# Rotations behind a projection's last rows, gates between the latent norms' steps, a new first stage, and modulation steps moved

## The reference, cut to what matters

```
def adaln(c, w, b):                      # shift, scale, gate (twice in the second block)
    return split(silu(c) @ w + b)        # w: 1024 x 6144 in the second block, 1024 x 3072 in the first
h = rmsnorm(x) * g * (1 + scale) + shift
q, k = rope(h @ w_q), rope(h @ w_k)      # "even" layer of the first block; rotations of q and k
cq = rmsnorm(h @ w_cq); ckv = rmsnorm(h @ w_ckv)       # "odd" layer: two latent vectors with norms
q = cq @ w_qb;  k, v = ckv @ w_kvb;  gate = silu(h @ w_gm)
x = x + g_m * (gate * attention(q, k, v)) @ w_out
x = x + g_f * (silu(h @ wg) * (h @ wu)) @ wd           # second block only
```

## Time and profile before

| | us |
|---|---|
| median of 3 runs (2638.52 to 2640.34) | 2638.56 |
| profiled execution, device time | 2641.35 |
| its span | 2639.6 |
| PE busy in the span | 2372.5 |
| DVE busy | 1290.1 |
| ACT busy | 780.2 |
| POOL busy | 403.9 |

### The profile page before, as it was taken

How to read it: one execution, slowest core, us unless ns; L and a number is a source line. 1 busy time by engine, 2 the same in 40 slices (tenths; PEclk the granted TensorE clock), 3 DMA queues, 4 the chain that set the end, 5 groups by cost and what they waited for, 6 DMA issues and landing times.

```text
span 2639.6 us, 30486 instructions
## 1 busy us (share of the span) xinstructions
PE 2372.5 (90%) x11834; PEld 1805.6 (68%) x11834; DVE 1290.1 (49%) x2860; ACT 780.2 (30%) x1607; POOL 403.9 (15%) x377
## 2 busy tenths in 40 slices
PE   5789998989899998989998989999969788999996
PEld 5676566558545756777875768887757557788875
DVE  4546564651135445628567356664226962333322
ACT  1235201430111302622237322223323361222332
POOL 1320010002100121031010120003541003000154
PEclk9989999989899998999879999999969899999998
DMA  6110232000124063013410035553213101222221
GB/s 276 48 41 18 88 106 94 17 17 0 68 86 146 24 181 111 9 64 121 143 66 1 1 128 192 186 183 127 86 48 112 48 1 64 80 96 96 96 96 56
DMA packets 58124, 225.89 MB, mean 86 GB/s; under 512 B 20462, under 2 KB 20974, under 8 KB 41468
## 3 DMA queue, kind: packets, MB, share of 16 engines
q1 hardware_dynamic: 57980, 223.94, 25.4%
HBM read 221.83 MB, written 2.10 MB: 85 GB/s over the span
## 4 chain that ended last, share of the span: by engine, by line
PE 77%; DVE 12%; POOL 3%; ACT 3%; issue 2%; DMA 2%; SPq 0%; POOLq 0%; DVEq 0%; ACTq 0%
PE PS L81 72%; PE PS L86 5%; DVE ACC L110 2%; DVE RINGr L98 1%; DVE WK L103 1%; POOL X L98 1%; DVE WK L152 1%; ACT WK L93 1%; ACT WK L91 1%; POOL WKr L98 1%; DVE WK L137 1%; DVE WK L110 1%; DVE SM L147 1%; DVE WK L98 1%; DMA WK<-in_rpb 1%
## 5 line engine op out<-in xcount | busy, mean ns | idle before, releaser
L81 PE MATMUL PS<-Hr,GBr 128*128 128x512 f32 x1280 | 441.0, 398 | 14.5 <-DVE RINGr L98 6.4
L81 PE MATMUL PS<-Hr,RINGr 128*128 128x512 f32 x1040 | 405.9, 390 | 0.0
L91 ACT ACTIVATE WK<-PS 128x512 f32<-128x512 f32 (+3 forms) x390 | 190.1, 518 | 524.4 <-PE PS L81 322.7
L81 PE MATMUL PS<-H,RING 128*128 128x512 f32 (+1 forms) x928 | 340.2, 518 | 0.0
L110 DVE SCALAR_TENSOR_TENSOR ACC<-ADA,SM,ACC 128x256 f32<-128x256 f32 x616 | 292.7, 499 | 74.7 <-DMA ACC<-in_l_mod_b 31.3
L81 PEld LDWEIGHTS PS<-Hr,GBr 128*128 128x128 f32 x1280 | 242.9, 191 | 73.1 <-POOL Xr L98 9.0
L98 DVE TENSOR_TENSOR RINGr<-RING,GBr 128x1024 fp32r<-128x1024 f32 (+1 forms) x155 | 201.2, 1337 | 184.2 <-ACT GBr L91 184.2
L81 PEld LDWEIGHTS PS<-H,RING 128*128 128x128 f32 x928 | 174.0, 192 | 136.8 <-issue 128.8
L81 PE MATMUL PS<-GBr,WKr 128*128 128x512 f32 (+1 forms) x774 | 249.5, 393 | 14.0 <-POOL WKr L98 12.7
L81 PE MATMUL PS<-RING,GB 128*128 128x256 f32 x1156 | 252.3, 381 | 4.8 <-DVE GB L115 2.2
L86 PE MATMUL PS<-CN,WK 128*128 128x128 f32 (+1 forms) x1152 | 185.9, 303 | 67.2 <-DVE WK L103 52.6
(11 more groups left out here) (175 smaller groups left out, 2911.6 us busy)
## 6 DMA issues: line engine op xcount, KB each, us to landing
ADA<-in_l_mod SPq DMA_DIRECT2D x96, 512.0 KB, 3.9
RING<-in_l_gu SPq DMA_DIRECT2D x44, 1024.0 KB, 4.9
RING<-in_l_wd SPq DMA_DIRECT2D x24, 1024.0 KB, 4.9
RING<-in_l_in SPq DMA_DIRECT2D x17, 1024.0 KB, 4.9
RING<-in_ev_in SPq DMA_DIRECT2D x13, 1024.0 KB, 5.8
ADA<-in_od_ada SPq DMA_DIRECT2D x24, 512.0 KB, 3.6
RING<-in_od_in SPq DMA_DIRECT2D x12, 1024.0 KB, 5.5
RING<-in_l_out SPq DMA_DIRECT2D x8, 1024.0 KB, 5.1
```

Source lines behind the costliest of these rows:

```text
L81: self.last = self.eng.matmul(out, lhsT, rhs, start=start, stop=stop, skip_group_check=True)
L91: self.last = self.eng.activation(out, in_, func, bias=bias, scale=scale)
```

## The change

- **First stage.** The two conditions, padded to 64 columns each, are the stationary operand; PE multiplies all 16 early chunks of shift and scale (groups 0 to 3 of four chunks), 16 matmuls of 256 columns a group, whose results go alternately to the lower and upper 64 partitions. ACT copies a group out, four matmuls with `pick` (two columns) turn it, DVE adds bias and norm gain. The diagonal of the norms replaces the scaled rows and the identity: x^T is a matmul of x with it, and `norm_tile` and the transposes of this stage are gone. The lower 4 column blocks are normalized while PE sums groups 1 and 3. DVE makes the 512 rows, ACT the 256. Loads: the small constants, x, groups 0 and 2, weight chunk 0, the lambda inputs, groups 1 and 3, chunk 1, the big tables, chunks 2 and 3.
- **Rotations** are called once behind both groups; the two `qr` behind the ckv spreads.
- **Odd layer.** ckv and kr come before the first sum of squares; the gate tiles 0 to 3 stand between the norms' steps (tiles 0 and 1 before the spread of cq, 2 before the ckv sums, 3 before kn).
- **Modulation steps.** 24 steps for groups 0 to 3 of the first layer are not in the list any more (they are in the new first stage). Calls: none behind the last vb tiles, none behind gm tile 7, `ada(4)` in proj N behind qd and kd and none behind vd. By the cursor, od group 3 is applied just before the odd layer's norm, and the steps of the second block come up to 12 chunks later: proj I does eight chunks instead of six, two of them behind its last tile.
- **FFN.** POOL's four additions stand behind slices 23, 25, 27 and 29.

```diff
 tensor, fm and fm_split:
                     pe.then_inc(pe_product, ("p", tag, t, s0))
-                    if then is not None:
-                        then(tag, t, s0)
+                if then is not None:
+                    then(tag, t)
...
+            def first_sums(grp):
+                b = next_bank(("first sums", grp), [(act_value, ("first sums", grp))])
+                for j in range(2):
+                    for kh in range(2):
+                        i = grp * 4 + j * 2 + kh
...
+                        for k in range(4):
+                            pe.matmul(half(bank(b, j * 256, j * 256 + 256), k % 2),
+                                      cpad[:, (kh * 4 + k) * 64:(kh * 4 + k) * 64 + 64], wv[:, k, :],
+                                      kh == 0 and k < 2, kh == 1 and k > 1)
+            def first_mods(grp):
+                pe.wait_ge(act_value, ("first sums", grp))
...
+                for f in range(4):
+                    pe.matmul(bank(7, ...), a[:, f * 128:(f + 1) * 128], pick, True, True)
+            def first_turned(f):
+                for gi, tl in enumerate((range(4), range(4, 6))):
...
+                        pe.matmul(bank(b, i * 128, (i + 1) * 128), Xt(t, f * 128, f * 128 + 128), length_at(t), True, True)
+            first_sums(0)
+            first_sums(2)
+            first_mods(0)
+            first_mods(2)
+            pe.wait_ge(x_in, "x")
+            for f in range(4):
+                first_turned(f)
+            first_sums(1)
+            first_turned(4)
+            first_turned(5)
+            first_sums(3)
+            pe.wait_ge(dve_value, ("first mods", 2))
+            first_mods(1)
+            first_mods(3)
+            first_turned(6)
+            first_turned(7)
 vector:
+            def norm_half(f0):
+                for f in range(f0, f0 + 4):
+                    first_norm(f)
+                    if f > f0:
+                        first_lower(f - 1)
+                first_lower(f0 + 3)
+            first_mods(0)
+            first_mods(2)
+            norm_half(0)
...
+            rest(0)
...
+            first_mods(1)
+            first_mods(3)
+            norm_half(4)
 tensor, proj B:
-                ada(4)
+                if j == 0:
+                    ada(4)
 tensor, proj M:
+            gates_m(FIRST["od_gm"], 0)
+            spread("cq", sqw(0, 0, 512), 512, [(dve_value, ("cqn", 1))])
+            fm(FIRST["od_in2"], 8, 0, "gm", 2, gated("gm", 2), LOC, Ht, h_od)
+            ada(3)
+            for key, a0, a1 in halves:
+                sum_squares(key, ...)
...
-                fm(i, 2, 4 + m, "qr", m, roped("qr", m), LOC, cq, cq_ready, rotate)
+                fm(i, 2, 4 + m, "qr", m, roped("qr", m), LOC, cq, cq_ready)
+            for key, a0, a1 in halves:
+                spread(key, ...)
+            for m in range(2):
+                rotate("qr", m)
+            fm(FIRST["od_in2"], 8, 1, "gm", 3, gated("gm", 3), LOC, Ht, h_od)
+            ada(3)
 tensor, proj N:
-                        ada(3)
+                        ada(4)
 gpsimd, ffn:
-                    if fz == 22:
-                        for t in range(4):
-                            add(wd, t, 0, t, WK[:, 6144 + t % 3 * 512:6656 + t % 3 * 512])
+                    if fz > 22 and fz % 2 and fz < 31:
+                        t = (fz - 23) // 2
+                        add(wd, t, 0, t, WK[:, 6144 + t % 3 * 512:6656 + t % 3 * 512])
 sync, proj M:
-            for j in range(4):
-                load()
-            for j in range(4):
-                ada(3)
-                ada(3)
-                load()
+            for loads, steps in ((2, 2), (1, 1), (1, 1), (2, 2), (1, 1), (1, 0)):
+                for j in range(loads):
+                    load()
+                for j in range(steps):
+                    ada(3)
```

More of the change, by code:

```diff
@@ L1036, in ffn @@
                         chunk_done(i)
[L1039 to L1048, removed]
-                        pe.wait_ge(ada_landed(2 * c + k // 4), ("ada_in", 2 * c + k // 4))
-                        pe.matmul(at, wv[k // 4][:, k % 4, f * 128:(f + 1) * 128], cpair[:, 2 * k:2 * k + 2], k == 0,
-                                  k == 7)
@@ L1055, in tensor @@
+            first_turned(7)
+            turn["set"] = list(range(8))
             close(of_pe, "norm ev")
@@ L1500, in scalar, with first_sums @@
                 act.activation(cond_th[key], vec(key, 0, 8), ACT.Tanh, scale=0.5).then_inc(act_value, ("cond", key))
+            act.wait_ge(x_in, "x")
+            for t in range(6):
+                act.activation(H[:, t * 1024:(t + 1) * 1024], Xt(t), ACT.Square, accum=ssq[:, t:t + 1])
+                act.then_inc(act_value, ("sq", "ev", t))
+            def first_sums(grp):
+                act.wait_ge(pe_product, ("first sums", grp))
+                a = ACC[:, grp % 2 * 512:grp % 2 * 512 + 512] if grp < 2 else GATE[:, grp % 2 * 512:grp % 2 * 512 + 512]
+                act.activation(a, bank(where["first sums", grp]), ACT.Copy).then_inc(act_value, ("first sums", grp))
@@ L1508, in scalar @@
-            round_h("ev", ((0, 512), (512, 768)))
+            first_sums(1)
+            first_sums(3)
+            for f in range(4, 8):
+                first_norm(f)
             close(of_act, "norm ev")
-            act.wait_ge(pe_turned, ("end", "norm ev"))
+            act.wait_ge(tables_in, "tables")
             for j in range(2):
@@ L2211, in vector, with gate_m @@
                 copy_out("cq", m, 0, 512)
+            def gate_m(t):
+                gate("gm", t, LOC)
+                if t < 7:
+                    ada(3)
+            for s0, n in ALLT:
+                copy_out("ckv", 0, s0, n)
             diagonal("cq", sqw(0, 0, 512), 512, 256)
+            rope("kr", 0, ALLT)
+            for t in range(2):
+                gate_m(t)
             for k in range(2):
@@ L2237, in vector @@
                 copy_out("vm", t, 0, 512)
-            for t in range(8):
-                gate("gm", t, LOC)
-                ada(3)
+            for t in range(4, 8):
+                gate_m(t)
             close(of_dve, "proj M")
@@ L2642, in gpsimd @@
             rope("kr", 0)
+            for t in range(3):
+                ada(3)
             power(("ckv", 0), n + 1, 4)
@@ L2646, in gpsimd @@
                 rope("qr", m)
-            for t in range(8):
+            for t in range(3, 7):
                 ada(3)
```

242 lines of the change are left out of this document (150 added, 92 removed).

## The result

| | before | after |
|---|---|---|
| median, us (4 runs each on one chip) | 2639.45 (2638.52 to 2643.19) | 2561.39 (2557.42 to 2563.05) |
| ratio to before, 95% interval | | 0.9699 [0.9683, 0.9716] |
| profiled execution; its span | 2641.35; 2639.6 | 2563.00; 2561.2 |

The change is faster by 78 us. The forecast was 2534 (105 less), its range ended at 2556: a miss of 27 us, on the slow side.

What follows compares the result with a forecast made beforehand. PE bounds the kernel gap by gap, with half clock after several gaps and DVE limiting in places. Stage gains less proj I's loss sum to 105.7 us, from 2641.35 to 2535.7; median 2532.9, plus 1 for collisions: 2534, range 2517 to 2556.

Steps and rivals of the forecast that it cites:

- First stage: Start of kernel: sums in alternating halves and new load order start the first projection near 48, not 85.64; gain 38 us.
- Rotations: Even layer's projections: 13 waits of PE for ACT's copy go, with half the restarts; gain 10.7 us.
- End of proj B: Apply and 9.37 us of PE idle go, 1.0 stays, 2 for half clock; gain 12.2 us.
- Proj M: Odd layer: norm and rotation waits, half clock and most end idle go, 2 of new waits; gain 22.4 us.
- FFN additions: Both FFNs: spreading POOL's four additions removes PE's 5.40 wait and 3.4 of half clock; gain 15.6 us in all.
- Proj N: 2.9 us of wait inside goes, end wait 4.67 falls to 0.7, some clock returns; gain 8.8 us.
- Proj S: Apply that waited 4.38 finds its sum, half clock goes, one chunk more for DVE; gain 3.5 us (-3 to 8).
- Proj I: Two more chunks and their loads behind the last tile delay the index scores; loss 5.5 us (4 to 8).
- Rival 5: Whole kernel: the change moves waits and PE only waits elsewhere; half the gain, 2587 us; chance 0.03.
- Rival 2: Proj M's waits replaced by DVE's chunks between norms, 10 us more, proj S at -3: 2551 us; chance 0.15.
- rival 3: First stage 10 us worse and Rival 2's losses in proj M and S together: 2561 us; chance 0.05.

Runs made afterwards that it cites:

- e7: Changed kernel with first-stage conditions padded to 128 columns, all sums in one place, no alternating halves: 2572.1 us.
- e4: Changed kernel with rotations called between a tile's two groups again (qr ones stay behind the ckv spreads): 2573.9 us.
- e1: Changed kernel with every call of the modulation steps back where it was before the change: 2565.1 us.
- e8: Changed kernel with proj M's order of before in all engines, modulation calls still behind gate tiles 0 to 6: 2578.5 us.
- e6: Changed kernel with POOL's four additions in a row behind slice 22 again: 2571.0 us.
- e3: Changed kernel with calls of five steps behind every tile of output projections ev, od, l0, and one instead of two behind proj S's first eight tiles: 2559.7 us.
- e5: Changed kernel with five steps behind tiles 0 to 2 of output projections od and l0 only, one instead of two behind proj S's first eight tiles: 2538.8 us.
- e9: Changed kernel with calls of 3, 3, 1, 0 steps behind proj I's four tiles, the rest in FFN 1: 2556.4 us.
- e10: Changed kernel with no call behind slice 0 of either FFN and calls of 3, 3, 3, 1 steps in proj I: 2555.0 us.
- e12: Kernel of e11 with two steps instead of three behind slice 1 of both FFNs: 2533.9 us.
- e11: Changed kernel with three-step calls behind early od and l0 output tiles, fewer steps in proj S, slice 0 of both FFNs and proj I: 2544.6 us.
- e2: Changed kernel with six steps instead of three behind slices 6, 9 and 12 of FFN 0: 2558.8 us.

## Why the prediction was wrong where it was

**First stage: right.** 37.05 against 38. The halves bring a factor 1.77 / 1.08 = 1.64 a chunk (e7; forecast 1 / 0.56 = 1.8), and the first chunk was there at 13.62, so that the rest followed as drawn: the first projection at 48.59, forecast 48. The Trainium skill ("TensorEngine Tiling (Array Packing)", Theoretical Speedup) allows up to 2 for 64 columns; the trace shows less.

**Rotations: right.** 12.25 against 10.7: the restart of 0.25 counts in full, of which I had taken half. A wait of 1.27 at 264.99 that comes with them (e4) had no term.

**End of proj B: right in size,** 11.4 (e1) against 12.2. The idle time and the apply give 10.2 of it (9.24 + 1.84 less the 0.93 that stay), so about 1.3 is left for the clock, where I had 2.

**Proj M: the sum is right, its two parts are not.** 22.0 against 22.4. The new order gives 17.9 (e8), where I had 10.5 + 6.0 - 2 = 14.5: no wait of PE of more than 0.5 us is left between the norm and the end of the stage, so the 2 kept for new ones were not needed. The steps taken from its end give 3.7 (e1), where I had 7.9. Of those, the 3.0 of half clock lie behind the stage's last mark: 830.50 to 837.30 ran at 0.60 of full before and 749.83 to 756.60 at 1.00 after, 2.7 us, and the table has them in the next stage. That the column agrees to 0.4 is partly luck.

**FFN additions: right by the stages,** 7.2 and 7.4 against 7.8 each. The medians of e6 give 9.6 for both where the forecast had 15.6, so the size is less sure than the place.

**Proj N: over-rated.** The 8.8 are 2.9 inside, 4.0 at the end and 1.9 of clock. The end came (4.67 to 0.93). The 2.9 inside did not go, for the forecast had given no reason why it should: it was 3.76 in the profiled execution, with half clock behind it where the kernel before had none. By the table the miss is 3.1, and about 6 if the 2.7 that belong to proj M's term are taken out. In other executions of the same code the wait is 1.30 to 3.35 (last section), so part of this miss is one execution's. The cause of the wait is a gate group that begins with three chunks, and its bias row: POOL clears ACC for it only at 882.77, behind a mask that had waited 13.28 for its rows. With calls of three steps (e1) PE has two waits there, of 1.16 and 1.15, and the clock reads 1.00 behind them. Timeline of POOL, then DVE, after:

```profile
880.50 2.21 POOL L103 TENSOR_TENSOR WK<-WK,CN 128x960 f32<-128x960 f32 x1 [13.28 <-DMA WK<-in_rpb]
882.77 0.53 POOL L125 MEMSET ACC<- 128x512 f32 x1
```
```profile
886.61 6.07 DVE L115 SCALAR_TENSOR_TENSOR ACC<-ADA,SM,ACC 128x256 f32<-128x256 f32 x8 [11.91 <-DMA ACC<-in_l_mod_b]
```

**Proj S: the step that failed first.** I wrote that the apply "now finds its sum", 3.5 to the good. It was 5.4 to the bad (5.6 come back in e1, with the calls as before). The steps came seven chunks later, and other applies now met chunks just issued: 1.70, 0.70 and 4.86 us of waits and a half-clock stretch. I had counted how many chunks the stage gets (one more) and not which call each apply falls behind. At the last of the three, DVE begins its chunk at 1156.39 and ends it at 1158.44, and PE sums at 1158.49. Its bounds were -3 to 8. e3 and e5 confirm the place: with one step a tile the inner part of proj S is 12.4 us shorter than in the changed kernel.

**FFN 0: a loss I had no term for.** 5.9 us (7.2 less 1.26). It now begins with a gate group of three chunks; e9 makes the same loss in FFN 1 (7.4), e10 moves the wait by a slice, and e12 takes it away from e11 with one chunk fewer in the call.

**Proj I: right mechanism, under-rated.** 9.6 (e2), 8.8 (e9) against 5.5. I added two chunks and their loads (4.2 and some load time) but not the bias row's 3.29 and the half clock on 6.4 busy us behind it.

**Sum of the misses:** S 8.9, FFN 0 6.5, I 4.0, N 3.1, FFN 1 1.5, first stage 1, output ev 0.7, attention D 0.6, A and B 0.6, M 0.4: 27.3. The first four come with one part of the change, the moved steps, which the prediction priced at the places where they went away, and hardly where they arrived. FFN 1 holds four chunks and a bias row now and held none before, but loses little by it: e1, which has none there, is 0.6 shorter. Rival 5 comes nearest in kind, waits that move and turn up elsewhere; I had held DVE's busy share (1290 of 2640 us) against it, and that share is no argument. Its price, half of the whole gain, was too high, as only this part came to nothing. Rival 2 named proj S at -3 and put the rest of its price on proj M, where nothing of it came. That rival 3's 2561 is the measured time is luck: the first stage it had 10 worse was right. The range, too narrow by 5 us, took these terms as independent; they hang on one cause.

## What to carry to other kernels

A list of small steps that all engines share keeps its total work when a call is taken out: write down, for every call of every later stage, which steps land there, and price those calls in which a step that another engine waits for follows the work just issued. A busy share says nothing about cover. By e11 and e12 a call is covered if its own chain (row from DMA, work, next load) is shorter than the tile beside it: 8.2 us was free beside a slice of 11, 12.6 cost 7. Work moved into a stage where its engine has room belongs behind the first tiles: behind the last tile it cost 12 us a stage (e3), behind the last but one still 6 with four chunks (e5). And a load that stands in SP's list behind steps that wait for DVE is issued only when they are done (e3, 1112.14), so the next stage's loads must not be needed before that.

## What the runs showed of the hardware

The same code does not always take the same time. Up to output od the changed kernel, e2, e5, e6, e9, e10, e11 and e12 are the same program. The table gives PE's wait in proj N, the granted clock in the 6.8 us behind it, and the stretch from attention M to output od:

| | e10 | e6 | e2 | e11 | e12 | e9 | e5 | after |
|---|---|---|---|---|---|---|---|---|
| wait, us | 1.30 | 1.83 | 1.49 | 2.24 | 2.57 | 2.92 | 3.35 | 3.76 |
| clock behind it | 1.00 | 1.00 | 1.00 | 0.75 | 0.76 | 0.55 | 0.58 | 0.59 |
| stretch, us | 273.7 | 275.1 | 275.3 | 277.8 | 277.9 | 278.7 | 278.9 | 279.3 |

The longer ones are those where half clock followed the wait. From e6 (wait 1.83) to e9 (2.92), 1.1 us of wait more goes with 3.6 us of time. But the length of a wait alone does not tell whether half clock follows. A wait of 2.24 in e11 had it behind it. The 2.91 of the kernel before, 2.86 in the same place of e8 and 3.10 in FFN 0 of e10 had not. Windows of e11, then of e8 and of e10:

```profile
896.90:903.70 6.80, 6.73 (x21) 4.96 (x22) 0.61 (x2) 0.98 (x2) 0.00 (x0) 0.75 0.64 166
```
```profile
915.00:921.80 6.80, 6.71 (x29) 5.56 (x30) 0.64 (x2) 0.98 (x2) 0.00 (x0) 1.00 0.62 168
```
```profile
1500.80:1507.60 6.80, 6.79 (x30) 5.63 (x31) 6.66 (x10) 0.60 (x1) 0.00 (x0) 1.00 0.80 295
```

What decides it, and what decides the length of the wait from run to run, stays open; the bias row's way over POOL and the mask rows' DMA is the only part of the wait that the trace shows waiting for DMA. So a difference of 4 us between single profiled executions of this kernel is no evidence before this stretch and its clock are compared, and e6's two numbers (9.6 by medians, 14.6 by stages) show how far apart the two measures can be.
